# Seven of eight gate/up K-tiles in three passes, with their splitting and the work around it laid out anew

## The chip, the cores and the metric

One core of a Trainium2 chip runs the whole program. The metric is the device time of one launch in microseconds; the time given for the kernel before is the median of three runs. PE is TensorE, ACT is ScalarE, DVE is VectorE, POOL is GpSimd, SP is SyncE, which issues most of the transfers.

## The reference

Two layers, each a mixer of three attention branches and then a mixture of 16 experts on 512 rows of 1024 values, in fp32. The change touches the experts alone:

```python
gate = jnp.sum(jax.nn.one_hot(expert_id, N_EXPERTS) * weights[..., None], axis=2)
hid = jax.nn.silu(jnp.einsum('bsd,edf->bsef', h, w_g)) * jnp.einsum('bsd,edf->bsef', h, w_u)
hid = hid * gate[..., None].astype(hid.dtype)
return jnp.einsum('bsef,efd->bsd', hid, w_d)
```

Each row goes to 2 of 16 experts (d = 1024, f = 256); 128 rows are a full block of one expert, and what goes over it is put on overflow lists.

## The kernel before

**One expert.** The kernel takes one expert per turn of a loop, `for e in range(N_EXPERTS + 1)`, written out for each engine. PE in turn e: `gate_up(e)` multiplies the turned rows of expert e with the gate and up weights, 8 K-tiles of 128 x 512 into one bank; `turn_gathered(e + 1)` turns the gathered rows of the next expert with 8 transposes; `down(e - 1)` multiplies the hidden values of the last expert with the down weights, 12 passes in two halves c = 0 and 1; `turn_hidden(e)` turns the new hidden values with 2 transposes.

**Two ways to multiply.** A K-tile is either native fp32 (one matmul of line 1284, two records in the trace) or three passes in fp32r (`three`, lines 987 to 989): both operands are split into a high part, which ACT makes by copying to fp32r, and a low part, the difference, which DVE or POOL makes. Experts 0 and 1 have all 8 tiles native. From expert 2 on (`FIRST_SPLIT`) tiles 0 and 1 are native and 2 to 7 in three passes (`SPLIT_FROM = 2`). Down weights are split too; of each expert the low part of half 0 is made by POOL in two subtractions (`weights_lo`, L922), that of half 1 by DVE (`down_lo_half`, L2285).

**Pieces.** Expert weights are loaded in three pieces (part 0 is K-tiles 0 to 3, part 1 is 4 to 7, part 2 is down) into 9 slots, three experts ahead. A slot is asked for again when PE has used it. The wait `arrived(e, part)` counts both gate/up pieces of an expert together.

**Turn e on ACT:** Silu (L1778); the high parts of the next rows (`et_out(e + 1)`, L1662 to L1668); the left half of the result rows of expert e - 1 (`rows_down`, L1693); `weights_hi(e)`, the down weights' high parts (L1684 x2); `gate_up_hi(e + 2)`, three copies of 1024 values (L1675).
**Turn e on DVE:** the product with up (L2299); low parts of the next rows (L2267, L2270); right half of the result rows of e - 1 (L2309); high and low part of the turned hidden values (L2319, L2321); `down_lo_half(e)`; the lists (`route_over` in turn 0, `route_rows` in 1, `route_blocks` in 2 and 3); `gate_up_lo(e + 2)`, three subtractions of 1024 values (L2277).
**Turn e on POOL:** the gather of rows for expert e + 3 (L898), `weights_lo(e)`, then `add_rows(e - 1)` (L912), which needs both halves of the result rows.

**The lists.** `route_over` (L2188 to L2211) ends with the semaphore `w_ready`; PE waits for it in turn 1, after `gate_up(1)`, before the small matmuls of L1410. In turn 5 PE turns the overflow lists into slots with 16 small matmuls (L1422).

The order on every engine is that of the code; nothing is scheduled by a planner here.

## Time and profile before

| what | us |
|---|---|
| median of 3 runs | 1389.27 (1387.7 to 1389.38) |
| the profiled execution | 1387.39 |
| its span | 1385.6 |
| experts of the first layer, 519.8 to 683.3 in the trace | 163.5 |
| experts of the second layer, 1202.6 to 1366.1 | 163.5 |

A row of a timeline is: start (us from the start of the span), duration, engine, line, operation, tile written and tiles read, partitions x elements, count, and in brackets the idle time before it with what ended it. Durations on an engine overlap a little where instructions follow closely, so the step from start to start is what an instruction costs. Each native K-tile shows two PE records.

### The profile page before, as it was taken

What the parts mean: (1) busy time and instruction counts of PE and PEld (TensorE: products, weight loads), DVE (VectorE), ACT (ScalarE), POOL (GpSimd) and SP (SyncE); (2) the same over time, 40 slices, a digit from 0 to 9 for tenths busy, and PEclk for the clock granted to TensorE, in tenths of its full rate; (3) what the DMA queues carried; (4) which work ended last, traced back from release to release, by engine and by line L of the source; (5) the groups of instructions that cost most, each with busy time, mean ns of one, the idle gap of its engine ahead of it and who ended that gap; (6) DMA issues with size and microseconds to landing.
All of it is one profiled execution on the core that took longest, in us unless ns stands there. A gap on an engine that the chain in (4) does not pass through costs nothing.

```text
span 1385.6 us, 19946 instructions
## 1 busy us (share of the span) xinstructions
PE 1351.8 (98%) x6972; PEld 1046.3 (76%) x6972; DVE 892.1 (64%) x2057; ACT 580.0 (42%) x1238; POOL 761.6 (55%) x603
## 2 busy tenths in 40 slices
PE   7999999999999999999789999999999999999997
PEld 5788877777777876777577888777777778677774
DVE  4487866646684347988446787665566741588882
ACT  4323334343433135676343432434334321466761
POOL 4566654454345664567555576455444457546673
PEclk9999999999999999999989999999999999999999
DMA  5436422223222569999632242222223128699993
GB/s 155 131 93 175 128 71 87 62 78 105 84 67 67 203 269 349 354 371 369 135 116 76 61 137 78 79 77 72 83 90 90 62 76 291 238 368 365 357 345 87
DMA packets 115066, 225.35 MB, mean 163 GB/s; under 512 B 18666, under 2 KB 28324, under 8 KB 114958
## 3 DMA queue, kind: packets, MB, share of 16 engines
q1 hardware_dynamic: 102526, 198.64, 42.6%
q0 software_dynamic: 9936, 16.81, 5.3%
q10 hardware_dynamic: 2496, 8.52, 1.6%
q8 instruction: 60, 0.98, 0.3%
q14 instruction: 48, 0.39, 0.1%
HBM read 216.52 MB, written 31.25 MB: 179 GB/s over the span
## 4 chain that ended last, share of the span: by engine, by line
PE 92%; DVE 4%; POOL 1%; issue 1%; ACT 1%; DMA 1%; POOLq 0%; SPq 0%; DVEq 0%; ACTq 0%
PE bank L987 23%; PE bank L989 22%; PE bank L988 22%; PE bank L1284 5%; PE bank L1163 4%; PE bank L1175 3%; PE bank L1196 2%; PE bank L1244 2%; PE bank L1116 1%; PE bank L1186 1%; POOL w_lo L842 1%; PE bank L1129 1%; DVE probs L2003 1%; DVE mixed L1820 1%; PE bank L1254 1%
## 5 line engine op out<-in xcount | busy, mean ns | idle before, releaser
L836 POOL TENSOR_SCALAR w_hi<-raw 128x1024 fp32r<-128x1024 f32 (+2 forms) x142 | 149.8, 1055 | 409.3 <-PE bank L989 406.6
L842 POOL TENSOR_TENSOR w_lo<-raw,w_hi 128x512 fp32r<-128x512 f32 (+2 forms) x288 | 359.4, 1269 | 16.4 <-ACT w_hi L1732 4.6
L988 PE MATMUL bank<-w_hi,hT_lo 128*128 128x512 f32 (+2 forms) x696 | 258.7, 372 | 0.0
L987 PE MATMUL bank<-w_lo,hT_hi 128*128 128x512 f32 (+2 forms) x576 | 216.8, 376 | 2.0 <-DVE hT_lo L1828 1.0
L989 PE MATMUL bank<-w_hi,hT_hi 128*128 128x512 f32 (+2 forms) x576 | 211.7, 368 | 0.0
L987 PE MATMUL bank<-hT_lo,w_hi 128*128 128x512 f32 x384 | 159.4, 415 | 0.0
L989 PE MATMUL bank<-hT_hi,w_hi 128*128 128x512 f32 x384 | 150.7, 392 | 0.0
L988 PE MATMUL bank<-hT_hi,w_lo 128*128 128x512 f32 x384 | 150.2, 391 | 0.0
L988 PEld LDWEIGHTS bank<-w_hi,hT_lo 128*128 128x128 f32 x696 | 131.5, 189 | 20.2
L987 PEld LDWEIGHTS bank<-w_lo,hT_hi 128*128 128x128 f32 x576 | 108.7, 189 | 28.0 <-issue 8.5
L989 PEld LDWEIGHTS bank<-w_hi,hT_hi 128*128 128x128 f32 x576 | 108.6, 188 | 17.9
L987 PEld LDWEIGHTS bank<-hT_lo,w_hi 128*128 128x128 f32 x384 | 72.1, 188 | 32.9 <-issue 20.5
L989 PEld LDWEIGHTS bank<-hT_hi,w_hi 128*128 128x128 f32 x384 | 72.1, 188 | 16.4
L898 POOL DMA_INDIRECT probs<-normed_dram,slot_token x32 | 35.3, 1102 | 87.7 <-PE bank L1244 68.6
L922 POOL TENSOR_TENSOR work_low<-work,w_hi 128x512 fp32r<-128x512 f32 x44 | 69.3, 1595 | 24.0 <-ACT w_hi L1684 24.0
L988 PEld LDWEIGHTS bank<-hT_hi,w_lo 128*128 128x128 f32 x384 | 72.3, 188 | 12.4
L987 PE MATMUL bank<-oT_lo,w_hi 128*128 128x512 f32 x192 | 79.4, 414 | 0.5 <-DVE hT_lo L2061 0.5
L989 PE MATMUL bank<-oT_hi,w_hi 128*128 128x512 f32 x192 | 76.0, 396 | 0.0
L988 PE MATMUL bank<-oT_hi,w_lo 128*128 128x512 f32 x192 | 75.7, 394 | 0.0
L1587 ACT ACTIVATE probs<-probs,job_neg 128x256 f32<-128x256 f32 (+5 forms) x128 | 66.6, 524 | 14.1 <-DVE job_neg L1986 14.1
L1163 PE MATMUL bank<-work 64*128 64x256 f32 (+3 forms) x384 | 64.0, 438 | 0.0
L1284 PE MATMUL bank<-work,ptmp 128*128 128x512 f32 x136 | 62.5, 594 | 1.0 <-issue 1.0
(359 smaller groups left out, 2836.5 us busy)
## 6 DMA issues: line engine op xcount, KB each, us to landing
raw<-in_w_gate SPq DMA_DIRECT2D x48, 512.0 KB, 3.8
work<-in_w_ff_gate SPq DMA_DIRECT2D x46, 512.0 KB, 6.5
work<-in_w_ff_up SPq DMA_DIRECT2D x46, 512.0 KB, 8.7
work<-in_w_ff_down SPq DMA_DIRECT2D x23, 1024.0 KB, 8.6
raw<-in_w_in SPq DMA_DIRECT2D x40, 512.0 KB, 3.6
raw<-in_w_branch SPq DMA_DIRECT2D x24, 512.0 KB, 3.6
w_lo_raw<-in_w_ff_down SPq DMA_DIRECT2D x10, 1024.0 KB, 8.1
X<-in_w_ff_gate SPq DMA_DIRECT2D x20, 512.0 KB, 5.8
```

Of the source, the lines that this page charges most:

```text
L836: nc.gpsimd.tensor_scalar(w_hi[:, two, :, 0:w], raw[:, slot, :, 0:w], 1.0, 0.0, ALU.mult, ALU.add).then_inc(split_hi, 1)
L842: last = nc.gpsimd.tensor_tensor(w_lo[:, two, kk, 0:w], raw[:, slot, kk, 0:w], w_hi[:, two, kk, 0:w].bitcast(F32), ALU.subtract)
L898: nc.gpsimd.indirect_dma_start(out=gather_rows[:, e % 2, :], out_offset=None, in_=xn_dram, in_offset=bass.IndirectOffsetOnAxis(ap=rows, ax ...
L922: last = nc.gpsimd.tensor_tensor(down_low(e)[:, f, c * 512:(c + 1) * 512], rows[:, f, c * 512:(c + 1) * 512], w_hi[:, c, f, :].bitcast(F32 ...
L987: nc.tensor.matmul(out_ap, s_hi, m_lo, start=start, stop=False)
L988: nc.tensor.matmul(out_ap, s_lo, m_hi, start=False, stop=False)
L989: return nc.tensor.matmul(out_ap, s_hi, m_hi, start=False, stop=stop)
L1163: last = nc.tensor.matmul(S[m][:, cols], q[r, job.u, job.i * P:(job.i + 1) * P], k[r, keys], start=True, stop=True)
L1175: last = nc.tensor.transpose(T[0][:, col:col + P], prob_bufs[job.g % 3][:, mm, b * P:(b + 1) * P], ident[:, :])
L1196: last = nc.tensor.matmul(O[HD * m:HD * (m + 1), job.i * P:(job.i + 1) * P], v, p[:, m, b * P:(b + 1) * P], start=(b == 0), stop=(b == len ...
L1284: last = nc.tensor.matmul(G[e % 2][:, :], et[:, e % 2, rows], gate_up_piece(e, part)[:, :, kk, :], start=(kt == 0), stop=(kt == KT - 1))
L1587: last = nc.scalar.activation(p, p, ACT.Exp, bias=job_neg[:, g % 4, m:m + 1], scale=-1.0, accum_out=job_sum[:, g % 4, m:m + 1])
```

## The change

- `SPLIT_FROM` is 1: only K-tile 0 of each expert from 2 on is native, 1 to 7 go in three passes (14 tiles fewer native in each layer).
- High and low parts of gate and up are made by whole pieces: `gate_up_hi(e, part)` and `gate_up_lo(e, part)`, with 1536 values per partition for part 0 and 2048 for part 1, in place of three times 1024.
- On ACT part 0 of expert e + 2 comes right after `et_out(e + 1)`, before `weights_hi` and `rows_down`; part 1 is last in the turn. ACT also makes the high part of the hidden values (`hidden_hi`), ahead of part 1.
- On DVE the low part of part 1 is made a turn later: in turn e it is that of expert e + 1 (`gate_up_lo(e + 1, 1)`), where before it was that of e + 2. Then follow `gate_up_lo(e + 2, 0)`, `down_lo_half(e)`, `hidden_lo(e)` and last `rows_right(e - 1)`. In turn 0 `hidden_lo(0)` stands ahead of `route_over`.
- `route_blocks` moves from turns 2 and 3 to 3 and 5, the small matmuls on PE from turn 5 to 7, PE's wait for the list from 6 to 8.

The rest is renaming (`y_act`, `y_dve`, `hi_by_act`). The diff, cut to its core:

```diff
-FIRST_SPLIT, SPLIT_FROM = 2, 2
-SPLIT_PAIRS = (8 - SPLIT_FROM) // 2
+FIRST_SPLIT, SPLIT_FROM = 2, 1
...
-def split_pairs(e):
-
-    return SPLIT_PAIRS * (e - FIRST_SPLIT + 1)
+def split_parts(e):
+
+    return 2 * (e - FIRST_SPLIT + 1)
...
-        gu_hi_bufs = [[oT_hi[:, 0:2], oT_hi[:, 2:4], oT_lo[:, 0:2], oT_lo[:, 2:4]],
-                      [hT_lo[:, 0:2], hT_lo[:, 2:4], hT_hi[:, 4:6], hT_hi[:, 6:8]]]
+        gu_hi_bufs = [[oT_hi[:, 0:4], oT_lo[:, 0:4]], [hT_lo[:, 0:4], hT_hi[:, 4:8]]]
...
+        def high_of(e, part):
+
+            first = 0 if part else SPLIT_FROM
+            return (gu_hi_bufs[e % 2][part].rearrange("p k n -> p (k n)")[:, 0:512 * (4 - first)]
+                    .rearrange("p (h k n) -> p h k n", h=2, n=FF))
...
-                        pair = (kt - SPLIT_FROM) // 2
+                        first = 0 if part else SPLIT_FROM
                         if kt == SPLIT_FROM:
                             pe.wait_ge(et_dve, e + 1)
-                        if (kt - SPLIT_FROM) % 2 == 0:
-                            pe.wait_ge(gu_lo, split_pairs(e - 1) + pair + 1)
+                        if kk == first:
+                            pe.wait_ge(gu_lo, split_parts(e - 1) + part + 1)
                         last = three(G[e % 2][:, :], et_hi[:, e % 2, rows], et_lo[:, e % 2, rows],
-                                     pair_hi_of(e, kt)[:, (kt - SPLIT_FROM) % 2, :], gate_up_low(e, part)[:, :, kk, :],
+                                     high_of(e, part)[:, :, kk - first, :], gate_up_low(e, part)[:, :, kk, :],
...
                     if e >= 1:
                         down(e - 1)
-                    if e == 5:
+                    if e == 7:
                         pe.wait_ge(e_hot, 1)
...
-                    if e == 6:
+                    if e == 8:
                         pe.wait_ge(e_known, 1)
...
-            def gate_up_hi(e):
-
-                for part, kk, kt in split_tiles():
-                    if kt == SPLIT_FROM or kk == 0:
-                        act.wait_ge(arrived(e, part), loaded(e, part))
-                    nc.scalar.activation(pair_hi_of(e, kt).rearrange("p k (h n) -> p k h n", h=2),
-                                         gate_up_piece(e, part)[:, :, kk:kk + 2, :].rearrange("p h k n -> p k h n"),
-                                         ACT.Copy).then_inc(gu_hi, 1)
+            def gate_up_hi(e, part):
+
+                first = 0 if part else SPLIT_FROM
+                act.wait_ge(arrived(e, part), loaded(e, part))
+                nc.scalar.activation(high_of(e, part), gate_up_piece(e, part)[:, :, first:4, :], ACT.Copy).then_inc(gu_hi, 1)
...
+            def hidden_hi(e):
+                act.wait_ge(hid_turned, e + 1)
+                if e >= 2:
+                    act.wait_ge(down_done, 2 * (e - 1))
+                nc.scalar.activation(hid_hi[:, e % 2, :], T[e % 2][:, 0:FF], ACT.Copy).then_inc(hidT_hi, 1)
...
                         et_out(e + 1)
+                    if splits(e + 2):
+                        gate_up_hi(e + 2, 0)
+                    if 1 <= e < N_EXPERTS - 1:
+                        weights_hi(e)
                     if e >= 1:
                         rows_down(e - 1)
+                    if e < N_EXPERTS - 1:
+                        hidden_hi(e)
                     if e == N_EXPERTS - 1:
                         et_out(e + 1)
-                    if 1 <= e < N_EXPERTS - 1:
-                        weights_hi(e)
                     if splits(e + 2):
-                        gate_up_hi(e + 2)
+                        gate_up_hi(e + 2, 1)
...
-            def gate_up_lo(e):
-
-                for n, (part, kk, kt) in enumerate(split_tiles()):
-                    v.wait_ge(gu_hi, split_pairs(e - 1) + n + 1)
-                    nc.vector.tensor_tensor(gate_up_low(e, part)[:, :, kk:kk + 2, :].rearrange("p h k n -> p k h n"),
-                                            gate_up_piece(e, part)[:, :, kk:kk + 2, :].rearrange("p h k n -> p k h n"),
-                                            pair_hi_of(e, kt).bitcast(F32).rearrange("p k (h n) -> p k h n", h=2),
-                                            ALU.subtract).then_inc(gu_lo, 1)
+            def gate_up_lo(e, part):
+
+                first = 0 if part else SPLIT_FROM
+                v.wait_ge(gu_hi, split_parts(e - 1) + part + 1)
+                nc.vector.tensor_tensor(gate_up_low(e, part)[:, :, first:4, :], gate_up_piece(e, part)[:, :, first:4, :],
+                                        high_of(e, part).bitcast(F32), ALU.subtract).then_inc(gu_lo, 1)
...
+            def hidden_lo(e):
+                v.wait_ge(hid_turned, e + 1)
+                v.wait_ge(hidT_hi, e + 1)
+                nc.vector.tensor_tensor(hid_lo[:, e % 2, :], T[e % 2][:, 0:FF], hid_hi[:, e % 2, :].bitcast(F32),
+                                        ALU.subtract).then_inc(hidT_done, 1)
...
                         et_out(e + 1)
-                    if e >= 1:
-                        v.wait_ge(down_done, 2 * e)
-                        if e - 1 >= 4:
-                            v.wait_ge(y_out[l][(e - 1) % 4], 16 * ((e - 1) // 4))
-                        if e == 1:
-                            v.wait_ge(w_known, 1)
-                        nc.vector.tensor_scalar(xn[:, (e - 1) % 4, 512:1024], G[3][:, :], slot_weight[:, EXPERT_AT[e - 1]:EXPERT_AT[e - 1] + 1], None,
-                                                ALU.mult).then_inc(y_dve, 1)
+                    if splits(e + 1):
+                        gate_up_lo(e + 1, 1)
+                    if e == 0:
+                        hidden_lo(e)
+                        route_over()
+                    if splits(e + 2):
+                        gate_up_lo(e + 2, 0)
+                    if 1 <= e < N_EXPERTS - 1:
+                        down_lo_half(e)
                     if e == N_EXPERTS - 1:
                         v.wait_ge(hid_turned, e + 1)
                         nc.vector.tensor_copy(pT[:, e % 2, 0:FF], T[e % 2][:, 0:FF]).then_inc(hidT_done, 1)
                         et_out(e + 1)
-                    elif e < N_EXPERTS:
-                        v.wait_ge(hid_turned, e + 1)
-                        if e >= 2:
-                            v.wait_ge(down_done, 2 * (e - 1))
-                        nc.vector.tensor_copy(hid_hi[:, e % 2, :], T[e % 2][:, 0:FF]).then_inc(hidT_hi, 1)
-                        v.wait_ge(hidT_hi, e + 1)
-                        nc.vector.tensor_tensor(hid_lo[:, e % 2, :], T[e % 2][:, 0:FF],
-                                                hid_hi[:, e % 2, :].bitcast(F32), ALU.subtract).then_inc(hidT_done, 1)
-                    if 1 <= e < N_EXPERTS - 1:
-                        down_lo_half(e)
-                    if e == 0:
-                        route_over()
+                    elif 1 <= e < N_EXPERTS:
+                        hidden_lo(e)
+                    if e >= 1:
+                        rows_right(e - 1)
                     if e == 1:
                         route_rows()
-                    if splits(e + 2):
-                        gate_up_lo(e + 2)
-                    if e in (2, 3):
-                        route_blocks(e - 2)
-                    if e == 5:
+                    if e in (3, 5):
+                        route_blocks((3, 5).index(e))
+                    if e == 7:
```

**ACT, first layer, turns 0 and 1,** before (X is the slot of expert 2, oT_hi and oT_lo take its high parts):

```order
L1778 ACTIVATE sq<-bank 128x256 [waits gu_done]
L1662 ACTIVATE ptmp<-bank 128x512 [waits et_turned]
L1675 ACTIVATE oT_hi<-X 128x1024 [waits gate_up_in2] x2
L1675 ACTIVATE oT_lo<-X 128x1024
L1778 ACTIVATE sq<-bank 128x256 [waits gu_done]
```

and now:

```order
L1777 ACTIVATE sq<-bank 128x256 [waits gu_done]
L1658 ACTIVATE ptmp<-bank 128x512 [waits et_turned]
L1670 ACTIVATE oT_hi<-X 128x1536 [waits gate_up_in2]
L1694 ACTIVATE hT_lo<-bank 128x256 [waits hid_turned]
L1670 ACTIVATE oT_lo<-X 128x2048 [waits gate_up_in2]
L1777 ACTIVATE sq<-bank 128x256 [waits gu_done]
```

The high part of the hidden values (hT_lo<-bank) is new here and stands behind the copy that waits for the weights of expert 2.

**DVE, first layer, turn 0,** before (the first row is the high part of the hidden values, the second the low part, the third opens `route_over`):

```order
L2319 CAST hT_lo<-bank 128x256 [waits hid_turned]
L2321 TENSOR_TENSOR hT_lo<-bank,hT_lo 128x256 [waits hidT_hi]
L2188 SCALAR_TENSOR_TENSOR score<-bank,block_ids 128x16 [waits over_counted]
```

and now:

```order
L2292 TENSOR_TENSOR hT_lo<-bank,hT_lo 128x256 [waits hidT_hi,hid_turned]
L2191 SCALAR_TENSOR_TENSOR score<-bank,block_ids 128x16 [waits over_counted]
```

`route_over` stands as before behind the low part, which now waits for ACT.

**DVE, first layer, turn 2,** before, from the product with up to the last subtraction on weights:

```order
L2299 TENSOR_TENSOR sq<-sq,bank 128x256 [waits hid_turned,silu_done]
L2267 TENSOR_TENSOR ptmp_low<-bank,hT_hi 128x256 [waits et_hi_done,gu_done,et_turned]
L2270 TENSOR_TENSOR ptmp_low<-bank,hT_hi 128x512 [waits et_hi_done]
L2309 TENSOR_SCALAR mixed<-bank,slot_weight 128x512 [waits down_done]
L2319 CAST hT_lo<-bank 128x256 [waits down_done,hid_turned]
L2321 TENSOR_TENSOR hT_lo<-bank,hT_lo 128x256 [waits hidT_hi]
L2285 TENSOR_TENSOR w_lo<-w_lo_raw,w_hi 128x2x512 [waits down_hi]
L2277 TENSOR_TENSOR work_low<-work,oT_hi 128x2x2x256 [waits gu_hi] x2
L2277 TENSOR_TENSOR work_low<-work,oT_lo 128x2x2x256 [waits gu_hi]
```

and now:

```order
L2315 TENSOR_TENSOR sq<-sq,bank 128x256 [waits hid_turned,silu_done,dve_0]
L2270 TENSOR_TENSOR ptmp_low<-bank,hT_hi 128x384 [waits et_hi_done,gu_done,et_turned]
L2273 TENSOR_TENSOR ptmp_low<-bank,hT_hi 128x512 [waits et_hi_done]
L2280 TENSOR_TENSOR work_low<-work,hT_hi 128x2048 [waits gu_hi]
L2280 TENSOR_TENSOR work_low<-work,oT_hi 128x2x768 [waits gu_hi]
L2286 TENSOR_TENSOR w_lo<-w_lo_raw,w_hi 128x2x512 [waits down_hi]
L2292 TENSOR_TENSOR hT_lo<-bank,hT_lo 128x256 [waits hidT_hi,hid_turned]
L2301 TENSOR_SCALAR mixed<-bank,slot_weight 128x512 [waits down_done]
```

The subtractions on weights (L2280, L2286) moved ahead of the hidden values and of the result rows.

## Rows read from the trace of the kernel before

**Rows 1.** The page, part 4: shares of the chain of waits by engine.

```profile
PE 92%; DVE 4%; POOL 1%; issue 1%; ACT 1%; DMA 1%; POOLq 0%; SPq 0%; DVEq 0%; ACTq 0%
```

**Rows 2.** Window of one expert: length; busy PE, PEld, DVE, ACT, POOL; PEclk, DMA share, GB/s.

```profile
1294.38:1304.06 9.68, 9.68 (x46) 7.40 (x45) 8.46 (x11) 6.96 (x12) 6.96 (x4) 1.00 1.03 357
```

**Rows 3.** Timeline of PE, one expert of the second layer.

```profile
1303.90 1.88 PE L1284 MATMUL bank<-work,ptmp 128*128 128x512 f32 x4
...
1305.85 0.40 PE L988 MATMUL bank<-oT_hi,ptmp_low 128*128 128x512 f32 x1
...
1309.80 1.04 PE L1244 MATMUL bank<-ident,probs 128*128 128x128 f32 x8
```

**Rows 4.** Timeline of DVE, one expert of the second layer.

```profile
1294.21 0.75 DVE L2309 TENSOR_SCALAR mixed<-bank,slot_weight 128x512 f32<-128x512 f32 x1 [1.25 <-PE bank L989]
1294.87 0.41 DVE L2319 CAST hT_lo<-bank 128x256 fp32r<-128x256 f32 x1
1295.32 0.42 DVE L2321 TENSOR_TENSOR hT_lo<-bank,hT_lo 128x256 fp32r<-128x256 f32 x1
1295.66 1.26 DVE L2285 TENSOR_TENSOR w_lo<-w_lo_raw,w_hi 128x1024 fp32r<-128x1024 f32 x1
1296.84 3.46 DVE L2277 TENSOR_TENSOR work_low<-work,oT_hi 128x1024 fp32r<-128x1024 f32 x2
1300.22 1.21 DVE L2277 TENSOR_TENSOR work_low<-work,oT_lo 128x1024 fp32r<-128x1024 f32 x1
1301.36 0.41 DVE L2299 TENSOR_TENSOR sq<-sq,bank 128x256 f32<-128x256 f32 x1
1301.69 0.41 DVE L2267 TENSOR_TENSOR ptmp_low<-bank,hT_hi 128x256 fp32r<-128x256 f32 x1
1302.02 0.68 DVE L2270 TENSOR_TENSOR ptmp_low<-bank,hT_hi 128x512 fp32r<-128x512 f32 x1
```

**Rows 5.** Timeline of POOL, the subtractions of one expert in each layer.

```profile
551.82 2.53 POOL L922 TENSOR_TENSOR w_lo<-w_lo_raw,w_hi 128x512 fp32r<-128x512 f32 x2 [0.37 <-ACT w_hi L1684]
...
1294.56 3.53 POOL L922 TENSOR_TENSOR w_lo<-w_lo_raw,w_hi 128x512 fp32r<-128x512 f32 x2 [1.32 <-ACT w_hi L1684]
```

**Rows 6.** Timeline of DVE, first layer, beside the first of Rows 5.

```profile
553.15 2.28 DVE L2285 TENSOR_TENSOR w_lo<-w_lo_raw,w_hi 128x1024 fp32r<-128x1024 f32 x1
```

**Rows 7.** Timeline of ACT, turn 0 of both layers.

```profile
532.73 2.00 ACT L1675 ACTIVATE oT_hi<-X 128x1024 fp32r<-128x1024 f32 x2 [4.18 <-DMA X<-in_w_ff_up]
...
1215.84 2.01 ACT L1675 ACTIVATE oT_hi<-X 128x1024 fp32r<-128x1024 f32 x2 [4.53 <-DMA X<-in_w_ff_up]
```

**Rows 8.** Timeline of DVE, first layer, turn 0: low part, then `route_over`, first and last.

```profile
529.45 0.42 DVE L2321 TENSOR_TENSOR hT_lo<-bank,hT_lo 128x256 fp32r<-128x256 f32 x1
529.79 0.33 DVE L2188 SCALAR_TENSOR_TENSOR score<-bank,block_ids 128x16 f32<-128x16 f32 x3
...
532.65 0.36 DVE L2211 TENSOR_TENSOR score<-score,weight 128x64 f32<-128x64 f32 x2
```

**Rows 9.** Timeline of PE, turn 1 of both layers: the small matmuls behind `w_ready`.

```profile
536.13 1.85 PE L1410 MATMUL bank<-score,hT_lo 128*128 128x16 f32 x16
...
1218.88 1.85 PE L1410 MATMUL bank<-score,hT_lo 128*128 128x16 f32 x16
```

**Rows 10.** Timeline of DVE and of POOL, end of the first layer's experts.

```profile
679.52 0.69 DVE L2260 COPY ptmp<-bank 128x512 f32<-128x512 f32 x1
...
679.99 1.55 POOL L912 DMA_INDIRECT residual_dram<-mixed,slot_token x1 [4.75 <-issue]
```

**Rows 11.** Timeline of DVE, `route_blocks(0)` (first row) and the next product.

```profile
558.76 0.15 DVE L2243 SCALAR_TENSOR_TENSOR raw<-raw,rank 128x8 f32<-128x8 f32 x1
...
560.34 0.42 DVE L2299 TENSOR_TENSOR sq<-sq,bank 128x256 f32<-128x256 f32 x1
```

**Rows 12.** Timeline of PE after its longest idle time, start of the second layer.

```profile
695.87 3.67 PE L1012 MATMUL bank<-ident,mixed 128*128 128x128 f32 x16 [9.51 <-DVE mixed L1820]
```

**Rows 13.** Weight transfers of one line, 1230 to 1350: issue to landing.

```profile
DMA to landing us min/median/max: 4.7/7.5/11.4
```

More of the change, by code:

```diff
@@ L415, in in_runs @@
             return src.rearrange("a (j p k) n -> p (a j) (k n)", p=P, k=ROW_RUN)
-        def split_tiles():
-            return [(kt // 4, kt % 4, kt) for kt in range(SPLIT_FROM, KT, 2)]
         banks = [ctx.enter_context(nc.psum_tensor(f"bank{i}", [P, 512], F32)) for i in range(8)]
@@ L934, in add_last_rows @@
                     pool.wait_ge(y_out[l][e % 4], 16 * (e // 4))
-                    for c, ready in enumerate((y_act, y_dve)):
+                    for c, ready in enumerate((y_left, y_right)):
                         pool.wait_ge(ready, e + 1)
```

34 lines of the change are left out of this document (20 added, 14 removed).

## The prediction

> **What bounds the kernel now.** I read the chain of waits first: 92% of it is PE, 4% DVE, 1% each ACT, POOL and DMA [rows 1]. So only two things move the end: less work on PE, or a wait of PE that was not there. Then the window of one expert [rows 2]: a turn is 9.68 us and PE is busy in all of it at granted clock 1.00 (the level of 2.4 GHz); DVE is busy 8.46, ACT and POOL 6.96 each, and the DMA engines are full (share 1.03). The engine nearest to PE is DVE, with 1.2 us to spare. Then the timelines of one turn on PE, DVE and POOL [rows 3 to 6], and last the places where the change puts a new neighbour beside a wait [rows 7 to 11].
>
> **The sum is made** on the profiled execution (1387.39, of which 1385.6 is the span and 1.8 lies outside it); the same difference is then put on the median, 1389.27, which is 1.9 above it. 0.2% (2.8 us) is about what a measurement of this kernel can tell from no change.
>
> **A. Less work on PE: -4.8.** In [rows 3] the second pass of the first split tile starts at 1305.85 and the transposes behind the last pass at 1309.80: 17 passes in 3.95, 0.232 each, three passes 0.70. The first pass then began at 1305.62, so the two native tiles (four records) took 1305.62 - 1303.90 = 1.72, 0.86 each. A tile saves 0.17 (0.86 less 0.70 before rounding); 14 tiles in each of two layers make 28 x 0.17 = 4.8. All of it is on the path, and the turn becomes 9.53.
>
> **B. PE waits for `w_ready` in turn 1: +4.5.** Before, in turn 0, DVE made both parts of the hidden values itself and went on to `route_over`, from 529.79 to 532.65 + 0.36 = 533.01, 3.22 long [rows 8]. PE comes to the small matmuls at 536.13, with no idle time in front [rows 9]: 3.1 to spare. Now ACT makes the high part, and stands before it in the copy of expert 2's first piece, which waits for weights: ACT sat idle 4.18 until 532.73 in the first layer, 4.53 until 1215.84 in the second [rows 7]. From the landing: the copy of 1536 values 1.5 x 1.00 = 1.50 (two of 1024 took 2.00 [rows 7]), the hidden copy taken as DVE's 0.42 for a like tile, the low part 0.34 (529.45 to 529.79 [rows 8]), `route_over` 3.22: 5.48. `w_ready` comes at 538.2 and 1221.3, where PE arrives at 536.13 and 1218.88: waits of 2.1 and 2.4, together 4.5. Nothing later takes it back, since PE is the bound. If a landing moves by 1 us, so does each wait. DVE's and ACT's queues have nothing else behind these that PE wants sooner.
>
> **C. DVE's budget in the turns from 2 on: +10.0, between 0 and +14.** DVE's steps of a turn, from start to start [rows 4], sum to 8.49 (1294.21 to 1302.02, then 0.68). One of them was not DVE's own: of 1024 values a subtraction of weights costs 1.14 alone (1300.22 to 1301.36), two 2.28, but these two took 3.38. POOL's own two took 3.53 there [rows 5], where in the first layer they took 2.53. In the first layer it is DVE's down subtraction that took 2.28 [rows 6] for 1.26 [rows 4], beside POOL's work from 551.82 to 554.35. So when both engines subtract weights one holds up the other: once per turn, for 1.0 to 1.1. Alone DVE's work is 8.49 - 1.10 = 7.39.
> The change takes away the high part of the hidden values (-0.45, 1294.87 to 1295.32) and adds two things. By the steps for 256 and 1024 values, 0.33 and 1.14, a value costs 1.055 ns: `et_out` has 128 more (+0.13), and the weights now go as 1536 (1.68) and 2048 (2.22) in place of three times 1024 (3.42): +0.48. New sum alone: 7.39 - 0.45 + 0.13 + 0.48 = 7.55. If POOL holds DVE up for one of its subtractions (2.53 / 2 = 1.26) it is 8.81, under the turn of 9.53, and PE sees nothing. If for both, 10.07: 0.54 over.
> Which? Before, POOL's first subtraction fell on DVE's rows that read a bank (result rows, hidden values), and only the second on weights. Now these rows come last, and DVE has 2.22 + 1.68 + 1.18 = 5.1 of subtractions of weights in one piece, from about 2.5 after the end of gate/up. POOL is released by `weights_hi`, behind Silu, `et_out` and the new copy on ACT, at about 4: in the middle of that piece, with both its subtractions. I take it that both are in the way in many turns, most of all in the second layer, where POOL was held up before.
> The upper end, per layer: turns 2 to 13, 12 x 0.54 = 6.5; the lists on DVE, three pieces of about 1.6 (`route_blocks(0)` 560.34 - 558.76 = 1.58 [rows 11], the other two taken the same, an estimate) +4.7; less what can be late before PE notices. The nearest need is that of `hidden_lo(e)`: `down(e)` comes a turn and eight transposes (some 0.8) after the end of gate/up, at 10.3. DVE has it at some 7.9: product and `et_out` done at 2.5, then 5.1 and 0.34. Spare 2.4. Less also the small matmuls on PE in turn 7, taken as 1.85 like those of [rows 9], a turn in which PE itself is longer. 6.5 + 4.7 - 2.4 - 1.85 = 7.0 per layer, 14 in all. The lower end is 0. I take 5.0 per layer, +10.0, nearer to the upper end, because the spare is used up after some five turns and the order puts both subtractions on DVE's. What PE waits for then: the hidden values' low part before `down`, the low parts of part 1 in `gate_up`, or POOL's low part.
> The Trainium skill, SBUF — State Buffer, section "Who interferes with whom", bears on this: a DVE instruction with two inputs in SBUF contends with a GpSimd instruction that reads SBUF for a shared pair of ports, which is an exclusive lock, and the later one blocks fully; with one such input it does not. The trace agrees: the 2.28, 3.46 and 3.53 are each longer by about one whole instruction of the other. By that rule the two subtractions of POOL in one piece of DVE's both block, and the term goes towards 14; without it DVE is at 7.55 and the term is 0.
>
> **D. The last expert's rows in the first layer: +0.5, between 0 and 1.0.** POOL's scatter of expert 14 begins at 679.99, before which POOL had waited 4.75 [rows 10]. The right half now comes behind `et_out(16)`, that is after 679.52 + 0.69 = 680.2, and takes 0.66: 680.9, so the scatter and the one behind it start 0.9 later. Down of expert 15 covers part; I take half. In the second layer the place has more room and costs nothing.
>
> **At nothing.** ACT gets the hidden copy and half a copy of 1024 more (6.96 to about 7.6 of 9.53): hidden by PE. `rows_down` goes behind `weights_hi`, two copies later; the banks are wanted only at the next `down`, a turn off. The lists of `route_blocks` and the matmuls that use them move by up to two turns together, as does PE's wait; no work is added. Transfers stay the same in number. If these covers fail, it is the same wait of PE as in C.
>
> **Sum:** -4.8 + 4.5 + 10.0 + 0.5 = +10.2. Own time 1397.6, median 1399.5.
>
> **The rivals.**
> *R1, DVE stays in its budget* (C is 0). For it: even with one subtraction in the way it has 0.7 to spare, and the start of POOL's pair, at about 4, is my estimate, which a fraction of a us can shift. Against: the order of [rows 4] is gone and the two pieces now meet. -4.8 + 4.5 + 0.5 = +0.2: 1389.5. Chance 0.20.
> *R2, neither wait appears, the kernel is faster.* The copy before the hidden values need not wait if expert 2's piece lands over 2.1 and 2.4 earlier than in [rows 7], and DVE stays under 9.53. From that point only A and D are left: 1389.27 - 4.3 = 1385.0. Against: nothing in the change asks for that piece earlier, and the landings were 532.73 and 1215.84. Chance 0.06.
> *R3, the clock falls in the new idle time.* After 9.51 of idle time 16 transposes took 3.67 [rows 12], 0.229 each against 1.04 / 8 = 0.130: that is nearer to the level of 1.2 GHz. B puts 2 us of idle ahead of small matmuls. If they go at half the clock, 1.85 more, and a little behind them, 2.2 per layer: 1399.5 + 4.4 = 1403.9. Against: 2 us is much less than 9.5, and [rows 9] show no fall. Chance 0.08.
> *R4, weights come too late for ACT.* ACT asks for part 0 some 2.6 sooner (two copies of 1.00 and 0.66 of result rows came first). Landings take 7.5 median and 11.4 at most [rows 13], and the DMA engines are full [rows 2]. 1 to 2 us more: 1401. Chance 0.06.
>
> **How the numbers follow.** Forecast 0.60, R1 0.20, R2 0.06, R3 0.08, R4 0.06. The range: C's lower end gives 1389.5, its upper end 1399.5 + 4.0 = 1403.5, D's upper end and the room of B another 1.0: 1389.5 to 1404.5. Faster by over 0.2%: R2, 0.06; within 0.2%: R1, 0.20; slower: the rest, 0.74.
>
> **What would show it.** A: 14 x 2 records fewer of native tiles in each layer, and a turn of 9.53 where nothing waits. B: idle time of 2.1 and 2.4 on PE before the small matmuls, ended by DVE's score. C: DVE busy 9.5 or more in a window of one turn, subtractions of 1536 and 2048 at up to 2.9 and 3.5, and PE idle before `down` or within `gate_up`, ended by DVE or POOL; turns over 9.6 in the middle experts. D: the first layer's last scatter 0.5 later. R3: a granted clock under 1.00 behind B's wait. The prediction is wrong if B's idle is missing, or if turns of experts 3 to 13 are 9.53 with DVE's subtractions of weights at 1.7 and 2.2.

## The result and the profile after

| | before | changed |
|---|---|---|
| median of 6 runs each (us) | 1388.46 (1387.27 to 1389.38) | 1395.47 (1392.86 to 1396.87) |
| profiled execution (us) | 1387.39 | 1395.38 |
| its span | 1385.6 | 1393.6 |

The changed kernel is slower: ratio 1.0050, 95% interval 1.0037 to 1.0063, that is +7.0 us where +10.2 was forecast. The two profiled executions lie 8.0 apart, and the account below is made on them. (The forecast median of 1399.5 is 4.0 above the measured one: 3.2 is the difference itself, 0.8 the kernel before, whose median of six runs is 1388.46 and not 1389.27.)

The chain of waits of the changed kernel (part 4 of its page; before, [rows 1]):

```profile
PE 80%; DVE 11%; issue 3%; DMA 2%; POOL 1%; ACT 1%; SPq 0%; POOLq 0%; DVEq 0%; ACTq 0%
```

PE went from 92% to 80% and DVE from 4% to 11%: the end is now followed back through DVE. What PE waited for, in total us, times and longest:

```profile
PE bank L1008 <- DVE mixed L1823: 12.1, 4, 8.6
...
PE bank L1406 <- DVE score L2214: 4.3, 2, 2.2
PE bank L983 <- DVE hT_lo L2292: 3.1, 6, 1.2
```

The second and third row are new: `w_ready` before the small matmuls (L1406), once per layer, and the hidden values' low part (L2292) before `down`, three times per layer.

**Turn 1.** ACT, DVE and PE around the new wait in the first layer, then PE in the second (timelines; compare [rows 7 to 9]):

```profile
533.11 1.48 ACT L1670 ACTIVATE oT_hi<-X 128x1536 fp32r<-128x1536 f32 x1 [4.25 <-DMA X<-in_w_ff_up]
534.50 0.36 ACT L1694 ACTIVATE hT_lo<-bank 128x256 fp32r<-128x256 f32 x1
...
534.97 0.42 DVE L2292 TENSOR_TENSOR hT_lo<-bank,hT_lo 128x256 fp32r<-128x256 f32 x1 [5.58 <-ACT hT_lo L1694]
...
538.16 0.36 DVE L2214 TENSOR_TENSOR score<-score,weight 128x64 f32<-128x64 f32 x2
...
538.67 2.08 PE L1406 MATMUL bank<-score,hT_lo 128*128 128x16 f32 x16 [2.07 <-DVE score L2214]
540.58 1.95 PE L1240 MATMUL bank<-ident,probs 128*128 128x128 f32 x8
...
1226.80 1.93 PE L1406 MATMUL bank<-score,hT_lo 128*128 128x16 f32 x16 [2.19 <-DVE score L2214]
1228.58 1.07 PE L1240 MATMUL bank<-ident,probs 128*128 128x128 f32 x8
```

ACT sits 4.25 before the weights' copy, the hidden copy follows, DVE waits 5.58 for it, and the lists end at 538.5, after which PE starts. The eight transposes behind it take 1.95 in the first layer and 1.07 in the second. The granted clock shows why (windows of the first layer; PEclk is the third number from the end):

```profile
536.13:538.67 2.54, 0.47 (x3) 0.04 (x1) 2.20 (x15) 0.89 (x2) 0.00 (x0) 1.00 1.05 387
538.67:540.58 1.91, 1.91 (x16) 1.91 (x17) 1.52 (x1) 0.00 (x0) 0.00 (x0) 0.93 1.05 385
540.58:542.18 1.60, 1.60 (x9) 1.60 (x10) 0.50 (x2) 0.47 (x2) 0.00 (x0) 0.50 1.06 389
542.18:543.90 1.72, 1.72 (x7) 1.39 (x6) 1.26 (x3) 1.52 (x3) 0.60 (x1) 0.55 0.91 335
```

It fell to 0.50 (the level of 1.2 GHz) after PE had been idle 2.07 and then done 16 matmuls of 16 columns, and stayed there for some 3.4 us. The small matmuls themselves were nearly over by then (2.08 for 1.85); the time is lost in the transposes and the first passes of `down`.

**A turn of the middle experts.** Windows of two turns of the changed kernel, beside [rows 2]; then DVE and POOL in the same two turns, beside [rows 4, 5]:

```profile
616.44:625.96 9.52, 9.52 (x48) 7.58 (x46) 9.52 (x9) 7.44 (x11) 6.10 (x3) 1.00 1.05 373
625.96:635.53 9.57, 9.57 (x47) 7.57 (x46) 8.74 (x9) 7.45 (x11) 8.40 (x5) 1.00 1.03 367
```

```profile
613.21 0.42 DVE L2315 TENSOR_TENSOR sq<-sq,bank 128x256 f32<-128x256 f32 x1 [1.93 <-ACT sq L1777]
...
617.29 2.85 DVE L2280 TENSOR_TENSOR work_low<-work,oT_hi 128x1536 fp32r<-128x1536 f32 x1
620.06 2.31 DVE L2286 TENSOR_TENSOR w_lo<-w_lo_raw,w_hi 128x1024 fp32r<-128x1024 f32 x1
...
623.29 0.40 DVE L2315 TENSOR_TENSOR sq<-sq,bank 128x256 f32<-128x256 f32 x1
...
626.88 1.74 DVE L2280 TENSOR_TENSOR X_low<-X,hT_lo 128x1536 fp32r<-128x1536 f32 x1
628.55 2.32 DVE L2286 TENSOR_TENSOR work_low<-work,w_hi 128x1024 fp32r<-128x1024 f32 x1
...
632.30 0.42 DVE L2315 TENSOR_TENSOR sq<-sq,bank 128x256 f32<-128x256 f32 x1 [0.44 <-ACT sq L1777]
```

```profile
616.78 4.51 POOL L918 TENSOR_TENSOR w_lo<-w_lo_raw,w_hi 128x512 fp32r<-128x512 f32 x2 [1.35 <-ACT w_hi L1677]
...
627.89 4.13 POOL L918 TENSOR_TENSOR work_low<-work,w_hi 128x512 fp32r<-128x512 f32 x2
```

PE is busy throughout. DVE's step from product to product is 10.08 in the first turn, with both of its subtractions lengthened (2.85 and 2.31), and 8.57 of work and 0.44 idle in the next, where only one is (1.74 and 2.32). The rows are DVE's turns 8 and 9. The two kinds alternate up to there and not after: in both layers the subtraction of 1536 is lengthened in turns 1, 2, 4, 6 and 8, in 10 of 28 in all, and in none from turn 9 on, while that of 1024 is lengthened in every turn that has one (2.10 to 2.33). In turns 8 to 13 PE does not wait at all, and they take 9.49 to 9.63.

**The account** between the two profiled executions, from the starts of PE's groups:

| | forecast | measured |
|---|---|---|
| A: turns 2 to 15 without waits, 134.3 for 136.7 in each layer | -4.8 | -4.8 |
| B: small matmuls 9.17 and 9.29 after `gate_up(1)` began, before 6.94 and 6.95 | +4.5 | +4.6 |
| clock at half level behind B, first layer (turn 1 took 17.20, before 13.28; less B) | in a rival | +1.7 |
| C: waits in turns 3, 5, 7: 2.0 in the first layer, 2.8 in the second | +10.0 | +4.8 |
| D: last `turn_hidden` to the second layer's first transposes, 19.1 for 17.6; second layer -0.4 | +0.5 | +1.1 |
| the mixers, 0.3 in each layer | 0 | +0.6 |
| sum | +10.2 | +8.0 |

### The profile page after: what moved, and what is told of

It is laid out like the page before. It is cut to its first block, busy times and chain, and to the rows that moved or that the text cites. A ratio compares the mean times of both kernels' runs of the same rounds, so it can differ in the third digit from the quotient of the medians.

```text
span 1393.6 us, 19974 instructions
## 1 busy us (share of the span) xinstructions
PE 1350.7 (97%) x7000; PEld 1051.9 (75%) x7000; DVE 912.0 (65%) x1999; ACT 596.4 (43%) x1240; POOL 791.7 (57%) x603
## 4 chain that ended last, share of the span: by engine, by line
PE 80%; DVE 11%; issue 3%; DMA 2%; POOL 1%; ACT 1%; SPq 0%; POOLq 0%; DVEq 0%; ACTq 0%
PE bank L983 21%; PE bank L985 20%; PE bank L984 20%; PE bank L1159 4%; PE bank L1171 3%; PE bank L1192 2%; DVE work_low L2280 1%; PE bank L1112 1%; DMA X<-in_w_ff_up 1%; PE bank L1182 1%; PE bank L1240 1%; DVE work_low L2286 1%; PE bank L1280 1%; DVE probs L2006 1%; POOL w_lo L838 1%
## 5 line engine op out<-in xcount | busy, mean ns | idle before, releaser
L838 POOL TENSOR_TENSOR w_lo<-raw,w_hi 128x512 fp32r<-128x512 f32 (+2 forms) x288 | 359.1, 1267 | 16.4 <-ACT w_hi L1731 4.6
L918 POOL TENSOR_TENSOR work_low<-work,w_hi 128x512 fp32r<-128x512 f32 x44 | 88.9, 2042 | 3.5 <-ACT w_hi L1677 2.9
L894 POOL DMA_INDIRECT probs<-normed_dram,slot_token x32 | 49.2, 1538 | 60.3 <-PE bank L1240 35.0
L983 PE MATMUL bank<-work_low,hT_hi 128*128 128x512 f32 x126 | 56.4, 448 | 0.0
```

The lines of the kernel that those rows point to most:

```text
L838: last = nc.gpsimd.tensor_tensor(w_lo[:, two, kk, 0:w], raw[:, slot, kk, 0:w], w_hi[:, two, kk, 0:w].bitcast(F32), ALU.subtract)
L894: nc.gpsimd.indirect_dma_start(out=gather_rows[:, e % 2, :], out_offset=None, in_=xn_dram, in_offset=bass.IndirectOffsetOnAxis(ap=rows, ax ...
L918: last = nc.gpsimd.tensor_tensor(down_low(e)[:, f, c * 512:(c + 1) * 512], rows[:, f, c * 512:(c + 1) * 512], w_hi[:, c, f, :].bitcast(F32 ...
L983: nc.tensor.matmul(out_ap, s_hi, m_lo, start=start, stop=False)
```

## The experiments

All are timed against the kernel before on the same chip. Its median was 1388.5 beside the changed kernel; 1388.3 beside the three single steps other than the lists, and beside the kernel with zeros from GpSimd; 1387.8 beside the lists first, the three steps together and their variants; and 1388.2 beside the kernels with right halves on ACT. A difference between kernels of different groups can be off by these 0.2 to 0.7. "ratio" is to the kernel before, with its 95% interval, whose half width is 1.2 to 2.1 us.

The granted clock also falls in a place that has nothing to do with the change, at the end of the router just before the experts. The window is of the last experiment below, the kernel with the wait put back; PEclk is again the third number from the end:

```profile
515.15:518.57 3.42, 3.42 (x14) 3.03 (x14) 1.58 (x8) 0.00 (x0) 1.27 (x2) 0.50 0.03 7
```

Such a fall stands in 11 of the 28 layers traced (14 executions), in none of those of the two kernels compared above, with no idle time over 0.41 in the 3 us before it, and costs some 1.4. It explains part of the scatter between runs: where the hidden values go first on ACT, three of eleven runs took 1392.1 to 1392.2 at a mean clock of 0.991, seven of the others 1388.7 to 1389.9 at 0.992 to 0.994, and the traced one, which is of the three, has the fall in both layers.

### The three places of loss, one at a time

**The hidden values first on ACT.**

```diff
+                    if e == 0:
+                        hidden_hi(e)
                     if splits(e + 2):
                         gate_up_hi(e + 2, 0)
...
-                    if e < N_EXPERTS - 1:
+                    if 1 <= e < N_EXPERTS - 1:
                         hidden_hi(e)
```

> The changed kernel with one step moved on ScalarE: in turn 0 the high part of the hidden values is made before the copy that waits for expert 2's weights, in place of after it. Theory (the order on ScalarE makes w_ready late, and the idle time on TensorE makes the clock fall in the first layer): the idle time of 2.1 and 2.2 us before the small matmuls goes in both layers, the granted clock behind it stays 1.00, turn 1 of the first layer takes 12.55 again in place of 16.45 and that of the second 12.55 in place of 14.94; the changed kernel's 1395.5 falls by 6.3 to about 1389.2. Rival one (the clock falls there because of the small matmuls, not because of the idle time): the idle time goes and the clock still falls, 1.7 less gained, 1390.9. Rival two (w_ready is late because of the weights or the lists, whatever the order): idle time stays, 1395.5.

Measured: 1389.83, ratio 1.0012 (1.0003 to 1.0021), 5.6 less than the changed kernel. Turn 1 takes 13.25 and 13.26, nothing stands before the small matmuls, and the transposes behind them take their 1.07 (second layer). The clock did not fall behind them, so it is not the small matmuls alone that bring it down there. Of the 6.3 expected 0.7 is missing: the wait in turn 3 of the first layer, 0.43 in the changed kernel, is now 1.23. The late turn 1 had given DVE time.

**The lists first on DVE**, with ACT's order as in the changed kernel:

```diff
                     if e == 0:
-                        hidden_lo(e)
                         route_over()
+                        hidden_lo(e)
```

> The changed kernel with one step moved on VectorE: in turn 0 the lists (route_over) come ahead of the hidden values' low part, while ScalarE still makes the high part behind the copy that waits for weights. Theory (w_ready is late only because the lists stand behind the low part): w_ready comes at about 532, no idle time before the small matmuls and no fall of the clock behind them, time as with the high part first, 1389.8. Rival (the hidden values' low part, now after both, becomes the wait: the down matmuls of turn 1 need it at 538.7): some idle time before these, 1391 or more.

Measured: 1389.44, ratio 1.0013 (1.0004 to 1.0022); turn 1 takes 13.24 in both layers, and the rival's wait before `down` did not come. The other way round gives the same: B is the product of two orders, DVE's and ACT's, and either of them undoes it.

**The result rows of expert 14 first in turn 15.**

```diff
                     if e == N_EXPERTS - 1:
+                        rows_right(e - 1)
                         v.wait_ge(hid_turned, e + 1)
...
-                    if e >= 1:
+                    if e >= 1 and e != N_EXPERTS - 1:
                         rows_right(e - 1)
```

> The changed kernel with one step moved on VectorE: in turn 15 the right half of the result rows of expert 14 is made first, as in the kernel before, not after the copies of hidden values and of the next rows. Theory (the late half sets the last scatters of the first layer): the scatter of expert 14 starts about 0.4 us after the start of the last expert's down matmuls in place of 2.4, the second layer's first transposes start 16.3 us after that in place of 18.0, and the time falls by 1.7 from 1395.5 to about 1393.8. Rival (only 0.7 of the 1.7 is order, the rest is a longer landing of the last scatter, which differs from run to run): it falls by 0.7 or less, to about 1394.8, and the landing stays near 3.6 in place of 2.6.

Measured: 1394.73, ratio 1.0044 (1.0030 to 1.0057), 0.7 less, though the trace shows 16.4 from the last down matmuls to the transposes in place of 18.0. Its profiled execution lost more in turn 1: 18.75 and 17.42 against 17.20 and 15.67, and less in turns 3, 5 and 7: 1.6 in both layers where the changed kernel lost 4.8, for the late turn 1 gave DVE time. Gains of 0.7 and of 1.7 cannot be told apart within the intervals, and a loss that differs by 3 us from execution to execution makes a size like D's unreadable here; the last series repeats it without that.

**The hidden values' low part ahead of the down weights'.**

```diff
                     if 1 <= e < N_EXPERTS - 1:
+                        hidden_lo(e)
                         down_lo_half(e)
...
-                    elif 1 <= e < N_EXPERTS:
-                        hidden_lo(e)
```

> The changed kernel with one step moved on VectorE: the low part of the hidden values stands before the subtraction of down weights, not behind it. Theory (VectorE is late only by the lists and only for the nearest need, the hidden values): the six idle times before the down matmuls in turns 3, 5 and 7 (0.24 to 1.24, 3.1 in all, with some 0.2 each for the restart) go, since half 1 of the down weights is wanted 1.4 later: 1395.5 falls by 4, to about 1391.5. Rival (VectorE's work is over its budget): TensorE waits for the down weights' low part or for gate and up in their place, and less than 1 is gained.

Measured: 1392.66, ratio 1.0029 (1.0017 to 1.0042), 2.8 less. The waits in turns 3, 5 and 7 are gone (9.49, 9.49 and 11.2 in both layers; so turn 7 of the changed kernel, 11.70, held one too). The theory said 4, the rival less than 1; the trace bears the theory out for the three turns. Turn 1 took 18.71 and 17.31 in this execution. In turn 15 PE waited 2.36 for DVE's subtraction of 2048 values, which took 5.84 for 2.28 with both of POOL's (3.08) inside it; a turn earlier ACT had waited 2.86 for gate/up weights (1.41 in the changed kernel). Which of the two brought the wait is open.

### Why DVE is late

> The changed kernel, but from expert 1 on GpSimd fills its half of the down weights' low part with zeros in place of subtracting: the part of GpSimd's that reads two tiles is left out, so the low part of half 0 of the down weights is missing from the products. Theory (the two engines' subtractions hold each other up): VectorE's subtractions of 1536 and 1024 values take 1.75 and 1.26 everywhere (now 2.85 and 2.3 where GpSimd works), VectorE is busy about 7.6 of a turn, the idle times in turns 3, 5 and 7 go; 1395.5 falls by 4.4 to about 1391. Rival (VectorE is slowed by something else, such as the transfers that fill the same turn): its durations stay at 2.3 to 2.85 and the time stays near 1395.5.

```diff
                         for f in range(2):
+                            if e:
+                                last = nc.gpsimd.memset(down_low(e)[:, f, c * 512:(c + 1) * 512].bitcast(F32), 0.0)
+                                continue
```

Measured: 1392.93, ratio 1.0037 (1.0023 to 1.0050), 2.5 less. The durations are the clear part; DVE's subtractions in one turn, and POOL's work beside them:

```profile
611.51 2.28 DVE L2283 TENSOR_TENSOR work_low<-work,hT_hi 128x2048 fp32r<-128x2048 f32 x1
613.71 1.75 DVE L2283 TENSOR_TENSOR work_low<-work,oT_hi 128x1536 fp32r<-128x1536 f32 x1
615.38 1.22 DVE L2289 TENSOR_TENSOR w_lo<-w_lo_raw,w_hi 128x1024 fp32r<-128x1024 f32 x1
...
613.17 0.99 POOL L919 MEMSET w_lo<- 128x512 f32 x2 [1.31 <-ACT w_hi L1680]
```

1.75 for 2.85 and 1.22 for 2.31, with the DMA engines as full as before (share 1.04 in this turn): it is POOL's subtractions, and not the transfers, that lengthen DVE's. The Trainium skill (SBUF — State Buffer, "Who interferes with whom") says that DVE's two-input instruction contends with a GpSimd instruction that reads SBUF and not with one that only writes it; the trace agrees, for the memsets run over the end of DVE's 2048 and the start of its 1536, and these take their 2.28 and 1.75. All turns from 2 on are at 9.50 and 9.57 here, so C was gone, all of its 4.8. The median fell by 2.5 only; the trace shows the clock as one cause, and whether it is all of it is open: turn 1 of the second layer took 17.47, and turn 1 of the first only 14.30, as PE came late to it and idled 0.79. What made it late is the fall of the clock at the end of the router.

### The three steps together, and the size of A

The first, third and fourth diff above in one kernel:

> The changed kernel with the three steps moved together: the hidden values' high part first on ScalarE in turn 0, the result rows of expert 14 first on VectorE in turn 15, the hidden values' low part ahead of the down weights' on VectorE. Theory (the three losses are separate and complete: w_ready, the hidden values' low part behind the lists, the last scatter): only the saving on TensorE is left, the turns are 9.57 and 9.49, no idle time in turns 1, 3, 5 and 7, 16.3 from the last expert's down matmuls to the second layer's transposes: 1388.3 less 4.8, 1383.5. Rival (taking one wait away hands VectorE's lateness to the next: without the wait in turn 1 it has less time and TensorE waits in turn 3 for the down weights or the gate and up): 1386 to 1388.

Measured: 1385.71, ratio 0.9989 (0.9980 to 0.9998). Faster than before, but 2 short. Turns 3 to 6 take 9.67, 9.98, 9.53 and 9.93, some 1.0 per layer over. In turn 4, PE's first pass of `down`, behind the transposes of 568.03, and POOL:

```profile
569.24 0.47 PE L983 MATMUL bank<-work_low,hT_lo 128*128 128x512 f32 x1 [0.17 <-issue]
...
561.36 1.59 POOL L908 DMA_INDIRECT residual_dram<-mixed,slot_token  x1 [2.60 <-DVE mixed L2303]
563.25 1.74 POOL L894 DMA_INDIRECT probs<-normed_dram,slot_token  x1 [0.30 <-issue]
565.02 4.12 POOL L918 TENSOR_TENSOR work_low<-work,w_hi 128x512 fp32r<-128x512 f32 x2
```

POOL waits 2.60 for DVE's half of the result rows, then scatters, gathers and subtracts until 565.02 + 4.12 = 569.14, and PE starts at 569.24 (the pass comes 1.21 after the transposes' start; 0.79 where nothing is late). The rival holds: DVE's lateness was handed to the next need, by way of POOL.

The same kernel with two native K-tiles again (`SPLIT_FROM = 2`):

> The kernel with the three steps moved, but with two native K-tiles per expert as before (SPLIT_FROM = 2), all else as in it. Theory (a native tile costs 0.17 more than three passes, 28 of them): turns of 9.74 and 9.66, 4.8 slower than with the three steps alone and equal to the kernel before, 1388.3. Rival (the arrangement itself costs or gains something beside the tiles): away from 1388.3 by over 1.5.

Measured: 1387.81, ratio 1.0000 (0.9991 to 1.0009). Turns are 9.74 and 9.68, as before, and no wait is left. So the new arrangement costs nothing by itself once the three steps are moved, and the one tile more is worth 2.1 there, and not the 4.8 that was expected. The traces give 2.8: 4.8 less the waits of 2.0, which DVE's added work brings (with the old split the lists fit in). The other 0.7 is within the intervals.

### DVE's budget from both sides

Right half of the result rows on ACT in turns 1 to 13:

```diff
+            def rows_right_act(e):
+                act.wait_ge(down_done, 2 * (e + 1))
+                nc.scalar.activation(xn[:, e % 4, 512:1024], G[3][:, :], ACT.Copy,
+                                     scale=slot_weight[:, EXPERT_AT[e]:EXPERT_AT[e] + 1]).then_inc(y_right, 1)
...
+                    if 1 <= e < N_EXPERTS - 2:
+                        rows_right_act(e - 1)
                     if splits(e + 2):
                         gate_up_hi(e + 2, 1)
```

> The kernel with the three steps moved, and in turns 1 to 13 the right half of the result rows is made by ScalarE (behind the hidden values' high part) in place of VectorE. Theory (VectorE's budget: 10.08 and 8.8 in alternate turns, mean 9.45 of 9.53, so the lists' 4.7 are not made up and TensorE waits 1.0 per layer in turns 3 to 6): VectorE's turn becomes 9.4 and 8.15, the lists are absorbed within a few turns, ScalarE is busy 8.1 of 9.53, all turns are 9.57 and 9.49, and the time is 2 less than with the three steps alone (1385.7): 1383.7. Rival (the 2 left over are not VectorE's work but the restart after each wait or the transfers): turns of 9.7 to 9.98 stay and the time stays near 1385.7.

Measured: 1383.61, ratio 0.9965 (0.9952 to 0.9979), 4.5 faster than before: nearly all of A's 4.8. Every turn from 2 to 14 is 9.5 to 9.6 (turn 7 with its matmuls 11.19), and DVE has room in the window of a turn while ACT, at 8.11, still has 1.5:

```profile
614.60:624.20 9.60, 9.60 (x47) 7.60 (x47) 8.86 (x9) 8.11 (x12) 8.02 (x5) 1.00 1.05 368
```

DVE keeps its budget although POOL is in its way more often than in the changed kernel: the subtraction of 1536 is lengthened in 18 of 28 turns, and in turns 6 to 12 of the first layer in a row. POOL and DVE in one of them:

```profile
610.91 4.52 POOL L918 TENSOR_TENSOR w_lo<-w_lo_raw,w_hi 128x512 fp32r<-128x512 f32 x2 [1.35 <-ACT w_hi L1677]
...
611.42 2.85 DVE L2288 TENSOR_TENSOR work_low<-work,oT_hi 128x1536 fp32r<-128x1536 f32 x1
...
614.53 1.98 DVE L2294 TENSOR_TENSOR w_lo<-w_lo_raw,w_hi 128x1024 fp32r<-128x1024 f32 x1
```

So the 9.4 and 8.15 in alternate turns that were expected did not come there; the time did, because DVE is under the turn of PE even with both in the way.

The other side: no native tile from expert 2 on (`SPLIT_FROM = 0`), first on the three steps, then on the kernel just shown.

> The kernel with the three steps moved and no native K-tile at all from expert 2 on (SPLIT_FROM = 0): TensorE saves another 0.17 per expert (turn 9.36), VectorE has 128 more values of the rows and 512 more of weights, +0.68. Theory (VectorE holds its budget only because GpSimd's two subtractions both fall on it in every second turn: 10.08 and 8.8 now, mean 9.45 of 9.53): the mean becomes 10.1, over 9.36, TensorE waits for VectorE in most turns: 0.6 for 12 turns in two layers, 14 slower than the three steps alone, about 1397. Rival (its budget has room, because GpSimd gives way and the two collide once a turn or less: 8.2 + 1.1): 4.7 faster, 1379.

Measured: 1398.97, ratio 1.0084 (1.0069 to 1.0099), 13.3 slower than the three steps alone, 14 expected. The number holds, the way to it does not: the loss is not 0.6 in most turns. In the first layer turns 3 to 7 take 11.1, 10.6, 11.7, 10.0 and 11.6, turns 10 and 13 take 10.4 and 10.2, and the others up to 14 take 9.3 to 9.4. The longest wait is 1.92 for DVE's subtraction of 2048 in turn 5.

> As the kernel with the right halves on ScalarE, but with no native K-tile from expert 2 on (SPLIT_FROM = 0). Theory (VectorE's budget): its turn is 10.1 with both of GpSimd's subtractions in the way and 8.85 with one, mean 9.5 over a turn of 9.36: 0.15 over in 12 turns plus the lists' 4.7 less the spare of some 3 come back as waits, about 3 per layer, against 4.7 saved on TensorE in both: about 1385. Rival (the waits of TensorE push the two engines apart, so that one collision a turn is left): 1379.

Measured: 1390.70, ratio 1.0018 (1.0008 to 1.0027): 7.1 slower than the kernel with one native tile, where 1.4 was expected. Turn 5 shows what the estimate lacked, DVE's subtraction and POOL's pair beside it:

```profile
572.76 4.90 DVE L2288 TENSOR_TENSOR X_low<-X,hT_hi 128x2048 fp32r<-128x2048 f32 x1
...
572.94 2.56 POOL L918 TENSOR_TENSOR work_low<-work,w_hi 128x512 fp32r<-128x512 f32 x2
```

Both of POOL's subtractions (2.56) fell on one of DVE's, 4.90 for 2.28, so that PE's gate/up passes waited 1.74. The mean of a turn does not catch this; turns 3 to 5 take 10.1, 10.4 and 11.6.

### D and B without the rest

Turn 15's order of the changed kernel again, all else as in the fastest:

> As the kernel with the right halves on ScalarE, but in turn 15 of VectorE the right half of expert 14's rows comes last again, as in the changed kernel. Theory (this order costs 1.3 to 1.7 in the traces, 18.0 in place of 16.3 from the last down matmuls to the transposes of the second layer): 1.5 slower, 1385.2. Rival (part of it is a longer landing of the last scatter that has nothing to do with the order): 0.7 slower or less.

Measured: 1384.88, ratio 0.9977 (0.9968 to 0.9986), 1.3 slower. From the last `turn_hidden` to the second layer's transposes it takes 19.0 in place of 17.8; the second layer gets 0.33 back, 0.9 net in the traces. D is real, and it is order: no run of the eleven is as fast as the slowest of the five without it (1384.13 against 1383.78). The changed kernel's own rows show how it comes about:

```profile
683.93 0.74 DVE L2301 TENSOR_SCALAR mixed<-bank,slot_weight 128x512 f32<-128x512 f32 x1
...
685.49 1.55 POOL L908 DMA_INDIRECT residual_dram<-mixed,slot_token  x1 [5.24 <-issue]
...
689.20 1.55 POOL L933 DMA_INDIRECT residual_dram<-mixed,half_token  x1 [0.30 <-issue]
694.41 0.68 POOL L832 TENSOR_SCALAR w_hi<-raw 128x584 fp32r<-128x584 f32 x1 [3.66 <-DMA residual_dram<-mixed,half_token]
```

The row of DVE ends at 684.7, POOL's scatter begins 0.8 later, and the last two come straight behind it. Before, the first began at 679.99 [rows 10], 0.4 after the last down matmuls had begun, and now 2.4.

B alone, with ACT's old order in turn 0 taken back:

> As the kernel with the right halves on ScalarE, but with the hidden values' high part behind the copy that waits for weights again in turn 0: the wait for w_ready alone, with no other loss to hide or feed. Theory (the idle time costs 2.2 per layer, and the clock behind it falls in most executions, 1.5 to 3.1 more in a layer where it does): 1383.7 + 4.5 + 2 to 5, about 1391.5, more spread from run to run than the kernel without the wait, turn 1 at 15.5 to 18.8. Rival (the clock's fall belongs to other stages and only the idle time counts): 1388.2.

Measured: 1392.18, ratio 1.0034 (1.0022 to 1.0047): 8.6 slower than without the wait. The forecast of 1391.5 holds, the rival's 1388.2 does not. The profiled execution is the fastest of the six (1390.4, 6.8 above that of the kernel without the wait) and shows 5.2 of it in turn 1: 14.45 in the first layer, with a wait of 0.94, and 17.25 in the second, 1.8 beyond its wait of 2.16. Another 1.4 is the fall of the clock at the end of the first layer's router, which is not of the wait's making. The untraced runs speak for the clock only by their mean: 0.989 to 0.993, the two slowest (1394.7 and 1394.8) at 0.989, where the five runs without the wait have 0.993 and 0.994. How much of their time was lost in turn 1 is not shown, nor is it that the wait makes the time scatter more: the spread is 4.4 here and 0.7 in those five runs, but 5.9 in the twelve of the three steps together, which have no such wait.

## Why the prediction was right, and where it was off

**A: right.** -4.8 in the traces, turns of 9.57 and 9.49, mean 9.53. The kernel with right halves on ACT shows it in the median (-4.5, with an interval of some 2 to either side).

**B: right, +4.6 for +4.5.** Both waits came, from the cause and with the rows named. Two kernels take them away from either side.

**The clock: a rival with a chance of 0.08 that came true in part.** "2 us is much less than 9.5" was the reason against it, and it was no reason: 9.5 was merely the only long idle time in the trace. In the traced executions the wait was 1.95 to 2.35 us eight times, and the clock fell behind seven of them, for 1.7 to 3.3 us each. It fell neither behind the two waits of 0.79 and 0.94 nor in the 18 other turns 1, which have no wait. R3 put most of the loss into the small matmuls; they lost 0.1 to 1.7, and the rest was lost behind them. This belongs into B as a term: 1.7, 4.9 and 5.0 in the three kernels traced with the full wait in both layers, 1.7 being the changed kernel's.

**C: the collision right, the term built on it wrong, +4.8 for +10.0.** The sum of a turn with both blocks was 10.07, and it is 10.08; the need that PE feels first, the hidden values' low part before `down`, is the one named, all six times. The step that failed is "both are in the way in many turns", carried over 12 turns as 12 x 0.54 = 6.5 per layer: from turn 3 to turn 8 both are in the way in every second turn, from turn 9 on in none. The mean of two turns is 9.3, under 9.53, and turns 8 to 13 lose nothing. In them R1 (DVE stays in its budget) is what happened. Why they alternate can be read from the rows, but no run tests it: `add_rows` on POOL waits for DVE's right half, which now comes last, so a late DVE holds up POOL, whose next pair of subtractions then starts later against DVE's (at 627.89, when DVE had begun its 1536 at 626.88) and lengthens one of them. This cannot be all of it, for in the kernel with right halves on ACT, where POOL does not wait for DVE's half, 1536 is free in turns 3 and 5 as well. What remains are three waits per layer, two turns behind each piece of the lists: 0.43, 0.46 and 0.24 in the first layer and 1.24, 0.48 and 0.26 in the second, some 0.25 each for the restart on top. That the lists bring them is read from their place; no run leaves the lists out. B and C are also not independent: the 3.9 lost in turn 1 of the first layer had spared DVE 0.8, and where turn 1 lost 5.5 there was no wait in turn 3 at all (9.52).

**D: direction right, size low.** +1.1 for +0.5, of +1.5 in the first layer. The scatter begins 2.0 later against the last down matmuls, where 0.9 was reckoned: the sum left out the 0.8 from the end of DVE's row to the start of POOL's scatter, which the middle turns show too (DVE's row ends at 602.65, the scatter begins at 603.49). Of the 2.0 a quarter is covered, and not half.

**At nothing: held.** ACT is busy 7.4, not late; `rows_down` and the moved lists cost nothing of their own. R2 and R4 fell: both waits came, and no wait of PE in the changed kernel's experts was for weights.

That the time lay in the range owes something to luck: B was exact, but C's excess of 5.2 stood against 3.0 that the sum had at nothing or too low (the clock 1.7, D 0.6, the mixers 0.6, B 0.1), with a cause for all but the mixers' 0.6.

## What to carry to other kernels

When a step is moved to another engine, look at what stands ahead of it in that engine's queue, and at what stands behind its consumer: here a copy of 0.36 us, put behind a wait for weights, held the lists of DVE and then PE. Where two engines take turns on a shared resource, a sum for the worst turn is not the sum for the mean; count in the trace how many turns have both. And a new idle time of the busiest engine is to be costed with what its clock does after it: here 2 us of it were enough for a fall that cost nearly as much again.

## What the runs showed of the hardware

- DVE's subtraction of two SBUF tiles and POOL's hold each other up: DVE's takes 2.85 for 1.75 and 2.31 for 1.22 with one of POOL's in the way (1.3 by itself), 1.98 for 1.22 in the kernel with right halves on ACT, and 4.90 for 2.28 where both of POOL's (2.56 together) fell on it. A memset by POOL over the same instructions does nothing to DVE's 2.28 and 1.75.
- The granted clock of PE fell to 0.50 after an idle time of some 2 us followed by 16 matmuls of 16 columns, in seven of eight cases; after 0.8 to 0.9 in neither of two, and with the same matmuls and no idle time in none of 18. At the end of the router it fell in 11 of 28 cases with no idle time over 0.41 in the 3 us before. What decides between the cases is open.
- In the first layer the landing of expert 2's first piece did not move with PE: where PE reached turn 1 some 1.3 to 1.4 later, ACT's copy still began at 533.12 and 533.39 (533.11 in the changed kernel), PE's wait was 1.1 to 1.3 shorter (0.79 and 0.94 for 2.07), and the small matmuls began at nearly the same time, 538.67 and 538.96 for 538.67.
